# A two-stack block on one Trainium2 core: attention scores issued ahead of the last pair's transposes, a product by pairs, and the recurrent layer's output product with its attention half first

## Chip, cores and metric

The kernel runs on one core of a Trainium2 chip. The metric is device time of one execution in microseconds (us); lower is better. The engines are named as in the profile: PE (TensorE), DVE (VectorE), ACT (ScalarE), POOL (GpSimd), SP (SyncE, here the queue that loads weights). About 0.2% (3 us) is what the measurement can tell from no change.

## The reference, cut to what matters

One sequence of 256 tokens, 1024 features, passes through a first stack of two layers. 16 learned tokens are then put in front (272 tokens) and a second stack follows: a recurrent layer with windowed attention, a feed-forward layer, a state-space layer, a feed-forward layer. Everything is float32. The change touches the mixing part of the first stack's layers and the recurrent layer:

```python
def first_block(x, ...):                      # two layers
    for l in range(DEPTH):
        proj = h @ w_in[l]                    # 1024 -> q, kv, gates, gla q/k/v/gate, pool inputs
        mixed = concatenate([
            nsa_mixer(...),                   # 6 query heads, 2 kv groups
            gla_mixer(...),                   # 6 heads of gated linear attention, times silu(og)
            pool_mixer(...)])                 # causal mean windows 2, 4, 8, 16
        h = layer_norm(ALPHA * h + mixed @ w_out[l], ...)
        ...
def nsa_mixer(q, kv, gates, ...):
    def compress(t, p, w1, w2):               # 15 blocks of 32 tokens
        hid = gelu(tb.reshape(B, G, n_cmp, 32 * 64) @ w1)
        return hid @ w2
    o = gate0 * softmax(q kc') vc + gate1 * softmax(q ks') vs + gate2 * softmax(q kw') vw
def griffin_swa_mixer(u, ...):                # the recurrent layer
    # gates x recurrence (rg_lru) beside windowed attention of 16 query heads
    # y = concatenate([gelu(gate) * rg_lru(conv(xr)), attention]) @ w_out
```

The selected branch takes every block at this length, so that it is plain causal attention, as the window branch is.

## The kernel before, in words

**Numbers and weights.** A float32 operand is kept as two float16 parts, a high and a low one, and a product of weights and operand is three matmuls for a block of 128 x 128 weights and up to 272 tokens: high x high, high x low, low x high (`split_matmul`, L656 to L658). Transposes, scores and values of the attentions are float32 matmuls. Weights stream through slots of 128 x 2048: SP loads a raw slot (four of them), ACT writes its high part (`high_part`, L1403), DVE its low part (`low_part`, L1969). Four split slots exist, so slot n+4 can be split only when the product of slot n is done. Such a split takes both engines in turn. The places where each engine splits the next slot are written out by hand as `give(n)`, `compression(n)` or by `product`.

**First stack, one layer.** The input product has 22 tiles of 128 outputs. Twelve or so come first; then PE's program weaves the rest into the attention. The attention works on six units p = 0 to 5 (three pairs of heads by two halves of 128 queries; units 3 to 5 see 256 keys and cost about twice as much). Unit p takes: `scores(p)` on PE (L950), `maxima(p)` on DVE (L2074, L2076), `exps(p)` on ACT (L1497), `weigh(p)` on DVE (L2082, L2085, L2087: one over the sum, times the branch's gate, times the probabilities), `turn(p)` on PE (transposes, L967), `copy_pt(p)` on ACT (L1506), `values(p)` on PE (L983), `copy_out(p)` on ACT (L1511). Scores live in banks 6 and 7 of PSUM, so scores(p+1) must wait for exps(p). Between them stand `compressed_hidden` (128 pairs of small matmuls for both compressed inputs), `compressed_keys`, `compressed_scores`, `compressed_turn` (L924), `pooled_out` (L992, then POOL's scaling of the residual, L2754) and the last input tiles T_PU (pooling) and T_OG (output gate of the linear attention). PE's order is turn(p), then scores(p+1), then a tile, then values(p).

**Output product and norm of a layer.** `out1` has eight tiles in four slots of two. The first four tiles are computed abreast, one row block of the operand after the other in `OUT1_ORDER`, so that work can begin before the last operand rows are there; the others follow tile by tile. The layer norm's sums are matmuls with a matrix of means (`mean_of`, L734), fed by DVE's evacuation of the tiles (L2010).

**Recurrent layer.** PE's program weaves 26 input tiles, 16 recurrence gates (`lru_gate`) and windowed attention of seven units (`scores`, `turn` L1184, `values`). DVE has for each unit `biased` (bias and maxima), `weight` and `mixed_low`; ACT has `exps`, `copy_turned`, `mixed_high`. The recurrence itself is one scan over 128 x 2176 on DVE (L2482), and `gated_out`, `gated_low` bring its result into the operand of the output product `out_g`, which has K = 16 row blocks: recurrence in the first eight, attention in the last eight. Its first four tiles are computed abreast over all 16 row blocks, and need four split slots at once. Tiles 4 to 7 follow.

## Time and profile before

| | |
|---|---|
| median of 3 runs | 1625.9 us (1624.11 to 1626.73) |
| profiled execution | 1623.0 us |
| its span in the trace | 1620.8 us |
| mean granted clock of PE | 0.932 |
| busy: PE, DVE, ACT, POOL | 1425.7, 1091.2, 819.6, 503.1 us |

The span is what the trace covers; 2.2 us of the profiled execution lie outside it. Busy times are sums of an engine's own work; an engine that is less busy may still be the one that others wait for, which the chain of waits tells. The granted clock is given in parts of 2.4 GHz: 1.00 is 2.4 GHz, 0.50 is 1.2 GHz. Line numbers are those of the kernel before.

### The profile page before, as it was taken

The numbers are of one execution on the slowest core, as the hardware profiler recorded it, in microseconds if no ns is written. First come the engines' busy times: TensorE is split into PE (matmuls) and PEld (weight loads), VectorE is DVE, ScalarE is ACT, GpSimd is POOL, SyncE is SP. The second block draws the span as 40 slices with busy tenths as digits, with TensorE's granted clock in tenths as the row PEclk, the third lists the DMA queues.
The fourth block names the chain that finished last, engine by engine and source line by source line (L and its number), as shares of the span: only waits on it lengthen the run. The fifth ranks groups of instructions, "written<-read, shape, count | busy, mean of one in ns | idle before, by whom it ended". The sixth has DMA issues, their size and how long they took to land.

```text
span 1620.8 us, 29305 instructions
## 1 busy us (share of the span) xinstructions
PE 1425.7 (88%) x12532; PEld 1190.8 (73%) x12532; DVE 1091.2 (67%) x1430; ACT 819.6 (51%) x1210; POOL 503.1 (31%) x390
## 2 busy tenths in 40 slices
PE   6988799989867999969878799997966986979997
PEld 4766688878746888857657688885845775868886
DVE  4864786566666774567846788657883666779863
ACT  5554454345463444447755555544661337555652
POOL 0132796131314991214200366301000111027630
PEclk9987899999979999989989899998986898989999
DMA  8530466545222566525324265552551122436650
GB/s 322 183 105 27 153 212 206 182 152 183 88 96 79 183 208 206 180 70 169 110 99 157 104 209 176 189 192 77 166 170 50 44 64 101 140 108 222 198 193 27
DMA packets 35697, 234.90 MB, mean 145 GB/s; under 512 B 4720, under 2 KB 6768, under 8 KB 8816
## 3 DMA queue, kind: packets, MB, share of 16 engines
q1 hardware_dynamic: 35568, 233.03, 42.0%
q8 instruction: 99, 1.62, 0.4%
q14 instruction: 30, 0.25, 0.0%
HBM read 231.97 MB, written 1.05 MB: 144 GB/s over the span
## 4 chain that ended last, share of the span: by engine, by line
PE 68%; DVE 15%; ACT 8%; issue 5%; DMA 1%; POOL 1%; SPq 0%; DVEq 0%; ACTq 0%; POOLq 0%
PE psum L656 20%; PE psum L657 20%; PE psum L658 20%; DVE low L1969 5%; ACT high L1403 3%; PE psum L734 2%; DVE arena L2331 2%; ACT arena L1497 1%; DMA raw<-stream 1%; PE psum L967 1%; DVE arena L2076 1%; POOL arena L2784 1%; PE psum L950 1%; DVE m L2029 1%; PE psum L1328 0%
## 5 line engine op out<-in xcount | busy, mean ns | idle before, releaser
L656 PE MATMUL psum<-u,high 128*128 128x256 f16 (+3 forms) x2296 | 644.2, 281 | 79.2 <-DVE u L2249 28.4
L1969 DVE SCALAR_TENSOR_TENSOR low<-raw,high 128x2048 f16<-128x2048 f32 (+3 forms) x230 | 522.9, 2280 | 231.0 <-ACT high L1403 230.9
L657 PE MATMUL psum<-u,high 128*128 128x256 f16 (+3 forms) x2296 | 643.4, 280 | 0.5 <-issue 0.5
L658 PE MATMUL psum<-u,low 128*128 128x256 f16 (+3 forms) x2296 | 642.5, 280 | 0.0
L1403 ACT ACTIVATE high<-raw 128x2048 f16<-128x2048 f32 (+3 forms) x230 | 415.2, 1811 | 136.8 <-PE psum L658 127.8
L656 PE MATMUL psum<-arena,high 128*128 128x256 f16 (+2 forms) x1136 | 314.8, 277 | 17.2 <-DVE low L1969 12.0
L656 PEld LDWEIGHTS psum<-u,high 128*128 128x128 f16 (+1 forms) x2296 | 228.3, 99 | 137.0 <-issue 82.9
L657 PE MATMUL psum<-arena,high 128*128 128x256 f16 (+2 forms) x1136 | 314.9, 277 | 0.0
L658 PE MATMUL psum<-arena,low 128*128 128x256 f16 (+2 forms) x1136 | 314.9, 277 | 0.0
L658 PEld LDWEIGHTS psum<-u,low 128*128 128x128 f16 (+1 forms) x2296 | 229.1, 100 | 37.1 <-issue 0.7
L657 PEld LDWEIGHTS psum<-u,high 128*128 128x128 f16 (+1 forms) x2296 | 228.6, 100 | 36.2 <-issue 0.9
L2711 POOL TENSOR_TENSOR arena<-arena 128x256 f16<-128x256 f32 (+1 forms) x108 | 168.8, 1563 | 8.5
L2709 POOL TENSOR_TENSOR arena<-arena 128x256 f32<-128x256 f32 (+1 forms) x108 | 129.2, 1196 | 111.4 <-DVE arena L2347 111.4
L2331 DVE SCALAR_TENSOR_TENSOR arena<-psum,par,arena 128x271 f32<-128x271 f32 (+3 forms) x296 | 142.5, 492 | 27.9 <-ACT arena L1688 13.7
L656 PEld LDWEIGHTS psum<-arena,high 128*128 128x128 f16 x1136 | 112.1, 99 | 36.2 <-DVE low L1969 12.9
L1389 ACT ACTIVATE arena<-psum 128x256 f32<-128x256 f32 (+3 forms) x138 | 52.1, 384 | 165.2 <-PE psum L658 125.9
L657 PEld LDWEIGHTS psum<-arena,high 128*128 128x128 f16 x1136 | 112.1, 99 | 16.8
L658 PEld LDWEIGHTS psum<-arena,low 128*128 128x128 f16 x1136 | 112.2, 99 | 16.2
L1688 ACT ACTIVATE arena<-psum,par 128x272 f32<-128x272 f32 (+1 forms) x88 | 49.4, 570 | 94.8 <-PE psum L658 93.3
L2784 POOL TENSOR_TENSOR arena<-arena 128x512 f32<-128x512 f32 x16 | 20.3, 1271 | 232.6 <-ACT arena L1908 232.6
L2719 POOL TENSOR_TENSOR m<-m,rstd 128x272 f32<-128x272 f32 (+1 forms) x12 | 11.1, 928 | 201.1 <-ACT rstd L1434 201.1
L2236 DVE TENSOR_TENSOR arena<-arena 128x256 f16<-128x256 f32 x64 | 46.6, 749 | 12.2 <-ACT arena L1389 12.1
(319 smaller groups left out, 1420.2 us busy)
## 6 DMA issues: line engine op xcount, KB each, us to landing
raw<-stream SPq DMA_DIRECT2D x208, 1024.0 KB, 4.8
raw<-stream SPq DMA_DIRECT2D x8, 768.0 KB, 4.3
con<-consts SPq DMA_DIRECT2D x1, 1746.0 KB, 12.3
raw<-stream SPq DMA_DIRECT2D x3, 512.0 KB, 3.7
raw<-stream SPq DMA_DIRECT2D x2, 712.0 KB, 5.9
h<-x_t SPq DMA_DIRECT2D x1, 1024.0 KB, 5.7
out_t<-h SPq DMA_DIRECT2D x4, 256.0 KB, 2.4
raw<-stream SPq DMA_DIRECT2D x1, 640.0 KB, 3.8
```

Of the source, the lines that this page charges most:

```text
L656: pe.matmul(out, w_hi, x[0], start=start, stop=False)
L657: pe.matmul(out, w_hi, x[1], start=False, stop=False)
L658: return pe.matmul(out, w_lo, x[0], start=False, stop=stop)
L1389: tell(act.activation(dst, bank(BANK[g], 0, n, rows), func, scale=scale / W_SCALE), *evac_value(g))
L1403: tell(act.activation(high[:, at:at + w], raw[:, off:off + w], ACT.Copy, scale=W_SCALE), high_ready if half != 0 else None)
L1688: tell(act.activation(buf[:, i % GATED, 0:outputs], bank(BANK[g], ahead, ahead + outputs), ACT.Identity, scale=pcol(f"ffn_w{l}", 2 * 2 * F ...
L1969: tell(dve.scalar_tensor_tensor(low[:, at:at + w], raw[:, off:off + w], W_SCALE, high[:, at:at + w], ALU.mult, ALU.subtract), split_ready ...
L2236: tell(dve.tensor_tensor(f1_hi[:, t, :], f_relu[:, t % 4, :], f_relu[:, t % 4, :], ALU.mult), fh_ready)
L2331: ins = dve.scalar_tensor_tensor(dst[:, lo:outputs], bank(BANK[g], at, at + n), weight(taps_in_all - 1 - back), dst[:, lo:outputs], ALU.mu ...
L2709: tell(pool.tensor_tensor(tmp[:, t % 2, 0:n], a[:, t % depth, 0:n], b[:, t % depth, 0:n], ALU.mult))
L2711: tell(pool.tensor_tensor(lo[:, t, 0:n], tmp[:, t % 2, 0:n], hi[:, t, 0:n], ALU.subtract), f_ready)
L2784: tell(pool.tensor_tensor(cd[:, q % 2], e2[:, q % 2], over(xbc[:, 24 + g, t0:t0 + n], 4), ALU.mult), cd_ready)
```

## The change

It changes the written orders of all engines in three places, and some of the work.

1. First stack: scores(p+1) stand ahead of turn(p). `compressed_hidden` is cut into its two inputs; the remaining tiles stand elsewhere, and all T_OG tiles use bank 0; the attention's output of units 3 to 5 uses bank 1. On ACT and DVE, exps(p+1), maxima(p+1) and the splits follow the new order. Gelu of the compressed hidden layer and Silu of the output gate are computed from Tanh with small DVE operations.
2. `out1`: the operand's parts have a home of their own (`g_hi`, `g_lo`), the first two tiles are abreast instead of four, the shift of the mean follows tile 2, and slots are split after each pair of tiles.
3. Recurrent layer: places of recurrence gates, exponentials, splits and of the scan change; the rows of `out_g` are reordered so that the attention stands in row blocks 0 to 7 and the recurrence in 8 to 15, and its slots hold tiles [0, 1] and [2, 3] with eight row blocks each.

```diff
-OUT1_BANKS = [0, 1, 6, 7, 2, 3, 0, 1]
+OUT1_BANKS = [0, 7, 6, 1, 2, 3, 0, 7]
-OUT1_ORDER = [6, 7, 3, 4, 5, 0, 1, 2]
+OUT1_ORDER = [3, 4, 6, 7, 5, 0, 1, 2]
@@ griffin_mix_rows
-    rows = list(range(D))
-    return rows + [D + (g * SWA_J + j) * HD + i for j in range(SWA_J) for g in range(2) for i in range(HD)]
+    rows = [D + (g * SWA_J + j) * HD + i for j in range(SWA_J) for g in range(2) for i in range(HD)]
+    return rows + list(range(D))
@@ slots of the stream
+            if name == "out_g" and i == 0:
+                for k0 in (0, 8):
+                    for both in ([0, 1], [2, 3]):
+                        steps.append((slot(name, 8 * 2 * P, k0, 8, tuple(both)), both, k0, 8))
+                i = 4
+                continue
@@ PE, first stack
                 one(T_PU)
+                scores(1)
                 values_to_tokens()
-                compressed_hidden()
+                turn(0)
+                compressed_hidden(0)
+                scores(2)
+                values(0)
+                turn(1)
+                compressed_hidden(1)
+                scores(3)
+                values(1)
+                turn(2)
                 one(T_PU + 1)
-                turn(0)
-                scores(1)
+                compressed_keys()
+                scores(4)
+                values(2)
+                compressed_scores()
+                turn(3)
                 one(T_OG)
-                values(0)
-                compressed_keys()
-                turn(1)
-                scores(2)
+                scores(5)
+                values(3)
+                turn(4)
                 one(T_OG + 1)
-                values(1)
-                compressed_scores()
...
+                compressed_turn(0)
+                values(4)
+                compressed_turn(1)
+                turn(5)
+                pooled_out()
                 one(T_OG + 2)
...
-                product(f"out1_{l}", x_at, ..., S, shift, late, OUT1_ORDER)
+                product(f"out1_{l}", lambda k: (g_hi[:, k, :], g_lo[:, k, :]), ..., S, shift, late, OUT1_ORDER, pairs=1)
@@ DVE, first stack
                 maxima(0)
                 weigh(0)
+                maxima(1)
...
+                give(7)
+                weigh(1)
+                maxima(2)
                 give(8)
+                low_part(matrices[f"cmp_{l}_0"] + SPLIT)
+                weigh(2)
...
+                tell(dve.scalar_tensor_tensor(t15, h15, GELU_CUBE, h15, ALU.mult, ALU.mult))
+                tell.settle()
+                tell(dve.scalar_tensor_tensor(t15, t15, 1.0, h15, ALU.add, ALU.mult), hid_summed)
+                maxima(3)
+                dve.wait_ge(hid_ready, l + 1)
+                tell(dve.scalar_tensor_tensor(h15, t15, 1.0, h15, ALU.add, ALU.mult), hid_gated)
@@ ACT, first stack
-                tell(act.activation(hid[...], hid[...], ACT.Gelu_apprx_tanh, scale=1.0 / W_SCALE), hid_ready)
-                act.preload_act_table_set("natural_log_exp_and_others")
+                tell(act.activation(hid_tanh[...], hid_tanh[...], ACT.Tanh, scale=GELU_ROOT), hid_ready)
@@ PE, recurrent layer
                 scores(0)
+                one(GQ[4])
                 for n in LRU_ORDER[8:11]:
                     lru_gate(n)
...
                 scores(1)
                 one(GQ[6])
+                for n in LRU_ORDER[14:16]:
+                    lru_gate(n)
                 one(GQ[7])
                 turn(0)
...
-                for step in steps[:4]:
-                    await_slot(step[0])
-                    for j in step[1]:
-                        bank_free(prod["first"] + j)
-                pe.wait_ge(sw_out, 5)
+                for j in range(4):
+                    bank_free(prod["first"] + j)
+                pe.wait_ge(sw_out, len(SWA_UNITS))
                 for half in range(2):
+                    for step in steps[2 * half:2 * half + 2]:
+                        await_slot(step[0])
                     for k in range(8 * half, 8 * half + 8):
-                        if k % 4 == 0:
-                            pe.wait_ge(y_split, min(3, 1 + k // 4))
-                        for step in (steps[half], steps[2 + half]):
+                        if half and k % 4 == 0:
+                            pe.wait_ge(y_split, k // 4 - 1)
+                        for step in steps[2 * half:2 * half + 2]:
@@ ACT, recurrent layer
-                recurrence_gates(8, 11)
                 exps(0)
                 query(4)
-                recurrence_gates(11, 14)
+                recurrence_gates(8, 11)
                 give(6)
                 query(5)
+                recurrence_gates(11, 14)
+                exps(1)
+                query(6)
                 recurrence_gates(14, 16)
@@ DVE, recurrent layer
-                biased(3)
-                tell(dve.tensor_tensor_scan(flat(gmix_a), flat(a_sc), flat(th), 0.0, ALU.mult, ALU.add))
...
                 mixed_low(4)
                 weight(6)
+                tell(dve.tensor_tensor_scan(flat(gmix_a), flat(a_sc), flat(th), 0.0, ALU.mult, ALU.add))
+                mixed_low(5)
                 give(11)
+                mixed_low(6)
```

**What stands where, three places.** Line numbers of the changed kernel differ: its scores are L958, turns L975, values L989, compressed turns L933, pooled product L998, low parts L1977, maxima L2083 and L2085, weigh L2091 to L2096.

PE in the first stack, before: compressed turns, then turn(3) (L967, eight transposes), scores(4) (L950), values(3) (L983), the pooled product (L992), turn(4), scores(5), values(4).

```order
L983 MATMUL psum<-arena 64x128 x4
L924 MATMUL psum<-con,arena 15x128 x8
L967 MATMUL psum<-con,arena 128x128 x8
L950 MATMUL psum<-arena 128x256 x4
L924 MATMUL psum<-con,arena 15x128 x4
L983 MATMUL psum<-arena 64x128 x8
L992 MATMUL psum<-m,misc 64x256 x4
L967 MATMUL psum<-con,arena 128x128 x8
L950 MATMUL psum<-arena 128x256 x4
L983 MATMUL psum<-arena 64x128 x8
```

PE at the same place after the change: scores(5) (L958), values(3) (L989), turn(4) (L975), then the tile T_OG+1 (24 matmuls of L666 to L668, left out), compressed turns (L933), values(4), turn(5) and the pooled product (L998).

```order
L958 MATMUL psum<-arena 128x256 x4
L989 MATMUL psum<-arena 64x128 x8
L975 MATMUL psum<-con,arena 128x128 x8
...
L933 MATMUL psum<-con,arena 15x128 x8
L989 MATMUL psum<-arena 64x128 x8
L933 MATMUL psum<-con,arena 15x128 x4
L975 MATMUL psum<-con,arena 128x128 x8
L998 MATMUL psum<-m,misc 64x256 x4
```

Scores(5) moved in front of turn(4), and the pooled product from between values(3) and turn(4) to behind turn(5).

DVE in the first stack, before: weigh(0) (L2082, L2085, L2087), a low part (L1969), maxima(1) (L2074, L2076), weigh(1), the next low part.

```order
L2082 RECIPROCAL arena<-arena 128x4
L2085 TENSOR_TENSOR arena<-arena 128x4
L2087 TENSOR_TENSOR arena<-arena 128x4x128
L1969 SCALAR_TENSOR_TENSOR low<-raw,high 128x2048
L2074 TENSOR_TENSOR psum<-psum,con 128x2x256
L2076 TENSOR_REDUCE arena<-psum 128x4
L2082 RECIPROCAL arena<-arena 128x4
L2085 TENSOR_TENSOR arena<-arena 128x4
L2087 TENSOR_TENSOR arena<-arena 128x4x128
L1969 SCALAR_TENSOR_TENSOR low<-raw,high 128x2048
```

DVE after the change: maxima(1) (L2083, L2085) stand before, and behind weigh(1) and maxima(2) two low parts (L1977) stand ahead of weigh(2).

```order
L2094 TENSOR_TENSOR arena<-arena 128x4
L2096 TENSOR_TENSOR arena<-arena 128x4x128
L2083 TENSOR_TENSOR psum<-psum,con 128x2x256
L2085 TENSOR_REDUCE arena<-psum 128x4
L1977 SCALAR_TENSOR_TENSOR low<-raw,high 128x2048 x2
L2091 RECIPROCAL arena<-arena 128x4
L2094 TENSOR_TENSOR arena<-arena 128x4
L2096 TENSOR_TENSOR arena<-arena 128x4x128
```

The low part that stood behind weigh(0) is now part of the two in front of weigh(2); maxima no longer wait behind it.

DVE in the recurrent layer, before: unit 3's biases (L2399) and maxima (L2402), then the scan (L2482, 128x2176), then a low part, mixed_low(1) (L2428) and weight(3) (L2420, L2422).

```order
L2399 SCALAR_TENSOR_TENSOR m<-con,psum 128x128 x8
L2402 TENSOR_REDUCE arena<-m 128x8
L2412 TENSOR_TENSOR arena<-arena,lnv 128x8
L2414 TENSOR_TENSOR arena<-par,arena 128x8
L2482 SCALAR_TENSOR_TENSOR arena<-arena 128x2176
L1969 SCALAR_TENSOR_TENSOR low<-raw,high 128x2048
L2428 TENSOR_TENSOR arena<-psum,arena 128x2x128
L2420 TENSOR_TENSOR arena<-arena 128x8
L2422 RECIPROCAL arena<-arena 128x8
```

DVE after the change: weight(6) (L2446, L2448), then the scan (L2521) between mixed_low(4) and the last low parts (L2454 is mixed_low, L1977 a low part).

```order
L2446 TENSOR_TENSOR arena<-arena 128x2
L2448 RECIPROCAL arena<-arena 128x2
L2521 SCALAR_TENSOR_TENSOR arena<-arena 128x2176
L2454 TENSOR_TENSOR arena<-psum,arena 128x2x128
L1977 SCALAR_TENSOR_TENSOR low<-raw,high 128x2048
L2454 TENSOR_TENSOR arena<-psum,arena 128x8x16
L2459 TENSOR_TENSOR arena<-arena 128x1088 x2
```

The scan moved from behind unit 3's maxima to behind the last unit's weight.

## Rows read from the trace of the kernel before

**Rows 1.** Page, part 4: shares of the chain that ended last, by engine.

```profile
PE 68%; DVE 15%; ACT 8%; issue 5%; DMA 1%; POOL 1%; SPq 0%; DVEq 0%; ACTq 0%; POOLq 0%
```

**Rows 2.** Windows by stage: length; busy PE, PEld, DVE, ACT, POOL (count); granted clock; DMA share; GB/s.

```profile
72.62:141.42 68.80, 53.86 (x644) 41.86 (x641) 42.73 (x68) 40.09 (x97) 16.41 (x10) 0.83 0.27 93
141.42:174.34 32.92, 29.38 (x216) 23.71 (x214) 14.76 (x18) 12.17 (x13) 6.29 (x6) 0.91 0.26 87
414.98:483.45 68.47, 51.49 (x630) 39.89 (x628) 42.58 (x66) 40.08 (x97) 16.40 (x10) 0.85 0.28 93
...
756.93:836.54 79.61, 61.55 (x487) 45.64 (x487) 60.96 (x95) 61.39 (x136) 15.64 (x9) 0.90 0.35 120
```

**Rows 3.** Windows at the lower granted clock, columns as in rows 2.

```profile
97.20:100.60 3.40, 3.40 (x18) 2.45 (x17) 2.99 (x3) 0.43 (x3) 3.32 (x2) 0.50 0.26 41
110.90:117.70 6.80, 5.43 (x25) 3.51 (x24) 4.17 (x5) 4.29 (x8) 0.00 (x0) 0.50 0.23 58
124.50:131.30 6.80, 5.88 (x32) 4.33 (x32) 4.76 (x4) 2.14 (x5) 1.09 (x1) 0.50 0.45 145
134.70:145.00 10.30, 10.14 (x65) 8.12 (x66) 5.15 (x15) 5.84 (x12) 0.00 (x0) 0.50 0.00 0
...
827.70:841.30 13.60, 6.50 (x34) 4.16 (x35) 6.92 (x7) 6.44 (x9) 0.00 (x0) 0.50 0.42 147
865.20:872.00 6.80, 5.30 (x24) 3.56 (x25) 6.76 (x6) 6.53 (x9) 0.00 (x0) 0.50 0.64 231
```

**Rows 4.** TensorE's waits, layer 0's attention, then layer 1's (total, times, longest).

```profile
PE psum L967 <- DVE arena L2087: 10.7, 3, 5.1
...
PE psum L967 <- DVE arena L2087: 12.8, 4, 5.1
```

**Rows 5.** The chain in layer 0's attention: start, us, what.

```profile
89.69 1.28 ACT L1577
...
121.56 2.32 DVE arena L2085
...
125.19 1.97 PE psum L967 x8
127.15 2.03 PE psum L950 x8
...
133.38 0.17 DVE arena L2085
...
134.86 1.97 PE psum L967 x8
```

**Rows 6.** The same chain: the two halves of a weight split.

```profile
93.92 1.93 ACT high L1403
...
95.87 3.02 DVE low L1969
```

**Rows 7.** Line L2754: ns min/median/max, first and last start.

```profile
L2754 POOL TENSOR_SCALAR m<-h x2: 5381/5382/5384, 120.2 to 464.3; 128x2048 f32<-128x2048 f32 x2
```

**Rows 8.** The chain in layer 0's output product.

```profile
162.67 2.81 DVE low L1969
```

**Rows 9.** Timeline of DVE behind the last values of layer 0.

```profile
142.25 1.09 DVE L1994 TENSOR_TENSOR u<-arena,u 128x256 f16<-128x256 f32 x3
```

**Rows 10.** TensorE's waits, recurrent layer, 757 to 840 us.

```profile
PE psum L656 <- DVE low L1969: 6.6, 2, 5.1
PE psum L1184 <- ACT arena L1750: 4.6, 1, 4.6
PE psum L1184 <- ACT arena L1752: 4.5, 1, 4.5
```

**Rows 11.** The chain at the recurrent layer's scan.

```profile
795.67 4.60 DVE arena L2482
```

**Rows 12.** TensorE's waits, recurrent output product, 840 to 900 us.

```profile
PE psum L656 <- DVE low L1969: 5.4, 1, 5.4
```

283 lines of the change are left out of this document (133 added, 150 removed).

## Prediction

> **What bounds the kernel now.** I read four views, in this order. First the page's chain that ended last: TensorE (PE) holds 68% of it, DVE 15%, ACT 8% and issue 5% [rows 1]. So time can be won only where PE waits or where it runs at the lower level of its clock. Then the same quantities by stage [rows 2]. In layer 0 of the first stack the attention stretch takes 68.80 us with 53.86 us of PE busy, and layer 1 takes 68.47 us with 51.49: PE idles 14.9 and 17.0 us. The output product and its norm take 32.92 us with 29.38 busy, so 3.5 idle. In the recurrent layer the gates, the windowed attention and the first matmuls of its output product take 79.61 us with 61.55 busy. The granted clock is 0.83 to 0.91 in these stretches: it is not only idle time that is lost.
>
> Third, the stretches in which the granted clock stands at 0.50, which is 1.2 GHz where 1.00 is 2.4 GHz [rows 3]. Each follows a wait of PE. In layer 0's attention they hold 3.40 + 5.43 + 5.88 us of PE busy and about 6.6 of the last row's 10.14 (the part before 141.42): 21.3 us. A matmul takes twice as long there, so up to 10.6 us are lost; I count 9.8, since the first and last matmuls of a stretch belong to the other level. The work of this attention is then 53.9 - 9.8 = 44.1 us at the full clock.
>
> Fourth, who ends PE's waits [rows 4] and the chain in one pair's round [rows 5]. Of layer 0's 14.9 us, 10.7 end with DVE's weigh (the scaling of the probabilities, L2087), all of them in front of a turn (L967); in layer 1 it is 12.8. The chain shows why. A turn starts at 125.19 and takes 1.97, then the next pair's scores take 2.03 (127.15), and only then can maxima, exponentials and weigh of that pair begin, so the next turn starts at 134.86: 9.67 us for a round in which PE has 4.0 us of turn and scores on the chain. In the late rounds no projection tile is left to fill the gap.
>
> **What the change does, part by part.**
>
> *First stack, attention (twice).* The scores of pair p+1 are issued in front of turn(p), and the interleaved projections and compressed parts are spread so that each round has one. The softmax of pair p+1 (from the end of the scores at 129.2 to the turn at 134.86 in the round shown, 5.6 us of maxima, exponentials and weigh) then runs beside values, turn and a tile of the pair before. Nothing is added on PE: the same matmuls, so 44.1 us of work. What takes the place of the old waits? Weight splits are queued on DVE in front of two of the weighs. In layer 0 ACT's half of a split takes 1.93 us now and DVE's 3.02 [rows 6]. Weigh(1) stands behind one split: I allow 1.1 us for turn(1). Weigh(2) stands behind two, the second of which needs ACT's half, which needs the slot that the first compressed product frees: 4 us, about one split of both engines (4.95) less what PE has to do meanwhile. For compressed keys, the last turns and the pooled product I add 3, together 8 where 14.9 stood. One gap of 4 us can bring the lower clock again; I allow 4 us of loss, where 9.8 is lost now. So 44.1 + 8 + 4 = 56.1 instead of 68.80: 12.7 won. In layer 1, with the same share of loss (9 us of 51.49), 42.5 + 12 = 54.5 instead of 68.47: 14.0. Together 26.7; I take 27. The ends: no wait and no low clock would give 14.9 + 9.8, less 5 that no order can hide, 20 a layer; with every round still waiting two thirds of what it waits now and the clock unchanged it is 4 a layer.
>
> *Table loads.* Gelu and Silu are replaced by Tanh with small operations on DVE, so that two of ACT's four table loads per layer go. One of them stood on the chain, 1.28 us at 89.69 [rows 5]. In the new order PE has other work at that place, so I count nothing extra, and up to 2.6 a layer as part of the upper end. The added DVE operations are about eight of four to thirty elements a row and three of 256; nearest row: the small one of 0.2 us on this chain, so some 2 us of DVE time, beside the last rounds, in which DVE waits.
>
> *POOL beside DVE.* POOL's scaling of the residual takes 5.4 us right after the pooled product, from 120.2 on [rows 7]. There it meets weigh(4): a four-element operation took 2.32 us (121.56), where the same operation takes 0.17 in the next round (133.38) [rows 5]. After the change the pooled product stands behind turn(5), so no weigh can meet it, and 2.1 us of today's wait go with it. It will meet the gating of the linear attention and the low halves of the operand instead. These have some 4 us of cover (compressed output, values(5), first five rows of the product). Price if the cover fails: up to 3 us a layer; I take 0. The Trainium skill's "GPSIMD Engine Reference", section "Key points", says that GpSimd shares its SBUF interfaces with VectorE, with contention for VectorE instructions with two SBUF inputs. That rule speaks against this placement, since the gating operations have two such inputs; the slow operation of the trace agrees with it, and by the rule alone the sum would be up to 6 us worse in the two layers.
>
> *First stack, output product (twice).* It now goes one pair of tiles abreast and then tile by tile, the shift of the mean comes after tile 2, and weights are split after every pair. At most the 3.5 us of idle go, and the low clock up to 145.0 (3.6 us, half of it lost, 1.8) [rows 3]: 5.3 a layer. Today DVE's half of a split stands on the chain there with 2.81 us, ahead of the evacuation of the last tiles [rows 8]. A new risk: with two tiles abreast instead of four, the five rows that are ready early cover 30 matmuls instead of 60 (216 take 29.38 us [rows 2], so about 3.5 us of them at the full clock). The last low halves end at 143.34, 1.9 us after the last values [rows 9], so they stay hidden. I take 5.0; ends 2 and 5.3. Two layers: 10.
>
> *Recurrent layer, middle.* The longest waits for turns and values there are 4.6 and 4.5 us [rows 10]. ACT's exponentials now come ahead of recurrence gates 14 and 15, whose product must be evacuated before turn(0) may use the bank; I get a stall of about 4.2 in front of turn(0) in place of the 4.5. With PE up to 2.6 us behind the old times at turn(2) and the scan of 4.60 (now in the middle of the weighs, at 795.67 [rows 11]) moved behind the last weigh, it recovers, and I count 0.
>
> *Recurrent layer, output product.* Its rows are reordered so that the attention half comes first. The first half now needs only two split slots, not four, and none of the recurrence. Today PE waits 5.1 us, the longest of the two for splits [rows 10], and starts at 836.54, where the last stretch of [rows 2] ends, at the lower clock, up to 841.3 [rows 3]. I get a start at about 831.7: 4.8 won and 2.4 of clock. The second half needs the recurrence, with the scan now late: its operand is ready at about 839.4 and its weights at 841.7 by my count, the first half ends at 843.0. This is close. Behind it the weights of tiles 4 and 5 can be split as soon as the first half is done, not after all four tiles: the wait of 5.4 [rows 12] goes, and the low clock after it (5.30 us of busy, half lost, 2.7). Sum 4.8 + 2.4 + 5.4 + 2.7 = 15.3. Two of these steps rest on margins of 1.3 and 3.6 us, so I take 11. Ends: -2 (the middle loses 2.6 and the second half waits for the scan) and 16.
>
> **The sum.** 27 + 10 + 11 = 48. The profiled execution took 1623.0 us (span 1620.8), so 1575.0; its time is 2.9 below the median of 1625.9, to which I apply the same difference: 1578. Bounds: 2 x (4 + 2) - 2 = 10 and 2 x (20 + 5.3) + 16 = 67.
>
> **Rivals.**
> *The full gain* (forecast): 40 to 60 won, 1566 to 1586; chance 0.57. For it: the waits are nearly all for one thing, which the new order takes off the path.
> *More than 60*, the clock at its full level through both attentions: under 1566; 0.08.
> *The weight splits take the place of the softmax.* Each round then keeps some 2 us of wait and its low clock; attention gives 4 to 5 a layer instead of 13. 9 + 10 + 11 = 30, time 1596; span 1586 to 1606; 0.20. For it: in layer 0 a split stood on the chain with 4.95 us, and the low stretches follow gaps of at most 5.1 us, while one of 4 remains by my count. The Trainium skill's "TensorE: Matmul & The Clock Gate", section "Why this matters for your kernels", asks for no idle gaps between bursts of matmuls, or the clock goes down to half; the stretches at 0.50 agree.
> *The recurrent layer gives nothing*: the second half waits for scan and gating, whose 4.60 us now come last. 37 won, 1589, span 1586 to 1592; 0.09. Against it: DVE is busy 60.96 of the 79.61 us, so it has room to catch up.
> *Slower.* Both halves of a split (1.93 + 3.02) come in front of every weigh, and the 24 matmuls beside them run at the lower clock: 4.95 + 1.3 in each of ten rounds, 62 lost against 48 won, 1640. It decides from 4.8 us a round on. Against it: only two of five rounds have a split queued in front. 0.04.
> *The change does nothing*, since the rounds are bound by DVE's own work: DVE is busy 42.73 of 68.80 us [rows 2], so hardly; 0.02.
>
> **How the numbers follow.** 0.2% (3 us) is about what a measurement of this kernel tells from no change. Faster 0.94, same 0.02, slower 0.04. The range takes the forecast, the recurrent rival, nearly half of the rival of the splits and a third of those over 60: 1563 to 1597.
>
> **What would show it.** Right: the attention stretches at 54 to 58 us with PE busy 46 to 49; the waits for weigh down from 10.7 and 12.8 to under 6, most of them in front of turn(1) and turn(2); no slow four-element operation in a weigh; the recurrent product starting five us earlier, with no wait for a split in its third pair. Wrong: a new long wait of TensorE for weigh or for recurrence gates 14 and 15; a granted clock that stays under 0.9 in the attentions; a wait for the gated recurrence in the middle of its product.

## The result, and the profile after

The changed kernel takes 1560.7 us (median of 4 runs, 1559.8 to 1562.0) against 1625.3 of the kernel before in the same runs: a ratio of 0.9603 (0.9591 to 0.9615). That is 64.6 us faster, where 48 were forecast, and 2.3 us below the lower end of the range. The profiled execution has a span of 1557.8 us, 63.0 less than before.

Where the 63.0 us come from is read from the starts of TensorE's groups of matmuls in both timelines. A stage ends where the next one's first matmul starts; "to the next product" includes the norm behind the output product.

| stage | before | after | won | forecast |
|---|---|---|---|---|
| up to the attention, layer 0 | 72.69 | 71.33 | 1.4 | 0 |
| attention, layer 0 | 68.80 | 52.46 | 16.3 | 13 |
| output product to the next product, layer 0 | 38.23 | 31.72 | 6.5 | 5 |
| feed-forward, layer 0 | 167.01 | 168.04 | -1.0 | 0 |
| input product of layer 1, up to its attention | 68.32 | 66.05 | 2.3 | 0 |
| attention, layer 1 | 70.30 | 51.40 | 18.9 | 14 |
| output product to the next product, layer 1 | 36.28 | 31.71 | 4.6 | 5 |
| feed-forward, layer 1, and input of the recurrent layer | 235.95 | 235.59 | 0.4 | 0 |
| recurrent layer, scores(0) to its output product | 78.96 | 77.74 | 1.2 | 4.8 |
| recurrent layer, output product | 53.76 | 43.70 | 10.1 | 10.5, with 4.3 held back from both |
| everything behind it | 730.5 | 728.1 | 2.4 | 0 |

The page of the changed kernel, part 4, the chain that ended last by engine:

```profile
PE 74%; DVE 13%; ACT 6%; issue 5%; POOL 1%; DMA 1%; SPq 0%; DVEq 0%; ACTq 0%; POOLq 0%
```

TensorE (PE) holds 74% of the chain where it held 68%, with 21 us less of busy time (1404.3 against 1425.7 for the same matmuls; the mean granted clock rose from 0.932 to 0.948): the rest of the 63.0 us is wait. By stage (length; busy PE, PEld, DVE, ACT, POOL with counts; granted clock; DMA share; GB/s), the answer to [rows 2]:

```profile
71.33:123.80 52.47, 48.37 (x642) 38.95 (x642) 44.26 (x70) 37.29 (x96) 15.34 (x10) 0.87 0.36 121
123.80:149.90 26.10, 26.09 (x214) 22.48 (x214) 17.71 (x23) 12.59 (x15) 6.57 (x7) 1.00 0.41 134
389.61:441.01 51.40, 46.91 (x642) 37.67 (x642) 44.06 (x70) 36.83 (x96) 15.45 (x10) 0.90 0.37 124
707.66:786.05 78.39, 63.02 (x487) 46.40 (x487) 54.15 (x90) 53.57 (x130) 19.92 (x9) 0.93 0.31 108
786.05:829.75 43.70, 43.41 (x373) 36.50 (x374) 31.14 (x33) 28.18 (x35) 0.00 (x0) 1.00 0.52 180
```

The last column but two is the granted clock. The two attentions have 4.1 and 4.5 us of idle PE where there were 14.9 and 17.0. Both output products run at a granted clock of 1.00 without a gap, and so does the recurrent output product. What PE waits for in layer 0's attention, then in layer 1's (total, times, longest), the answer to [rows 4]:

```profile
PE psum L904 <- issue: 1.7, 1, 1.7
PE psum L975 <- DVE arena L2096: 1.3, 1, 1.3
PE psum L958 <- DVE arena L2168: 0.5, 1, 0.5
...
PE psum L975 <- DVE arena L2096: 3.7, 2, 2.3
PE psum L958 <- ACT arena L1506: 0.3, 1, 0.3
```

L975 is the turn, L2096 weigh. The waits of 10.7 and 12.8 us in front of the turns are now 1.3 and 3.7. The 1.7 us without a releaser stand among the small matmuls of `compressed_hidden`. In the recurrent layer, up to the output product and at its start:

```profile
PE psum L1172 <- POOL m L2795: 5.6, 3, 3.6
PE psum L1172 <- ACT arena L1733: 4.5, 1, 4.5
PE psum L1189 <- ACT arena L1760: 2.0, 1, 2.0
...
PE psum L666 <- DVE arena L2454: 1.2, 1, 1.2
```

L1172 is the turn of this layer, L1189 its values. (Their lines before are L1167 and L1184: both waits at L1184 in [rows 10] stood in front of values, not of a turn.) The 5.4 us of [rows 12] are gone, and the 4.5 us in front of turn(0) are there as forecast (4.2). Grown is the first row: PE waits for POOL, at most 3.6 us at a time, where it waited 1.1 us in all before. The last row is what is left in front of the output product, where 5.1 us stood [rows 10].

The lower clock did not go away. In layer 0's attention it stands from 85.4 to 99.0 us (columns as above):

```profile
86.00:90.00 4.00, 3.63 (x101) 3.31 (x102) 3.81 (x4) 2.32 (x11) 0.00 (x0) 0.50 0.78 266
90.00:93.60 3.60, 1.87 (x43) 1.66 (x40) 1.93 (x1) 2.29 (x2) 0.00 (x0) 0.50 0.74 250
93.60:97.00 3.40, 3.40 (x21) 2.22 (x18) 3.14 (x12) 1.49 (x2) 0.00 (x0) 0.50 0.72 217
97.00:100.70 3.70, 3.70 (x27) 2.78 (x24) 3.67 (x5) 2.54 (x10) 0.00 (x0) 0.73 0.31 128
```

It begins during the wait of 1.3 us in front of turn(1) and holds over the wait of 1.7. The wait need not be its cause: the kernel with five edits, below, has the lower level at the same place and no wait there. The attention's busy time of 48.4 us is 4.3 above the 44.1 that I worked out for the full clock.

### The profile page after: what moved, and what is told of

It reads as the page before. It is cut to its first block, busy times and chain, and to the rows that moved or that the text cites. A ratio compares the mean times of both kernels' runs of the same rounds, so it can differ in the third digit from the quotient of the medians.

```text
span 1557.8 us, 29313 instructions
## 1 busy us (share of the span) xinstructions
PE 1404.3 (90%) x12532; PEld 1181.0 (76%) x12532; DVE 1091.9 (70%) x1442; ACT 815.7 (52%) x1210; POOL 506.7 (33%) x390
## 3 DMA queue, kind: packets, MB, share of 16 engines
q1 hardware_dynamic: 35568, 233.03, 43.7%
## 4 chain that ended last, share of the span: by engine, by line
PE 74%; DVE 13%; ACT 6%; issue 5%; POOL 1%; DMA 1%; SPq 0%; DVEq 0%; ACTq 0%; POOLq 0%
PE psum L666 22%; PE psum L667 22%; PE psum L668 22%; DVE low L1977 4%; ACT high L1408 2%; PE psum L744 2%; DVE arena L2357 2%; ACT m L1748 1%; POOL arena L2808 1%; PE psum L975 1%; DVE m L2038 1%; DMA raw<-stream 1%; DVE m L2425 1%; PE psum L1333 0%; PE psum L958 0%
## 5 line engine op out<-in xcount | busy, mean ns | idle before, releaser
L666 PE MATMUL psum<-u,high 128*128 128x256 f16 (+4 forms) x2168 | 606.7, 280 | 78.4 <-DVE u L2275 28.4
L1977 DVE SCALAR_TENSOR_TENSOR low<-raw,high 128x2048 f16<-128x2048 f32 (+3 forms) x230 | 517.9, 2257 | 226.6 <-ACT high L1408 226.4
L667 PE MATMUL psum<-u,high 128*128 128x256 f16 (+4 forms) x2168 | 606.0, 280 | 0.0
L668 PE MATMUL psum<-u,low 128*128 128x256 f16 (+4 forms) x2168 | 605.4, 279 | 0.0
L666 PE MATMUL psum<-arena,high 128*128 128x256 f16 (+2 forms) x1264 | 347.5, 275 | 8.2 <-DVE arena L2654 5.2
L667 PE MATMUL psum<-arena,high 128*128 128x256 f16 (+2 forms) x1264 | 347.5, 275 | 0.0
L668 PE MATMUL psum<-arena,low 128*128 128x256 f16 (+2 forms) x1264 | 347.5, 275 | 0.0
L666 PEld LDWEIGHTS psum<-u,high 128*128 128x128 f16 (+2 forms) x2168 | 215.2, 99 | 132.3 <-issue 80.1
L668 PEld LDWEIGHTS psum<-u,low 128*128 128x128 f16 (+2 forms) x2168 | 215.7, 99 | 33.8
L667 PEld LDWEIGHTS psum<-u,high 128*128 128x128 f16 (+2 forms) x2168 | 215.3, 99 | 33.9 <-issue 0.9
L666 PEld LDWEIGHTS psum<-arena,high 128*128 128x128 f16 x1264 | 123.8, 98 | 28.2 <-issue 7.9
L667 PEld LDWEIGHTS psum<-arena,high 128*128 128x128 f16 x1264 | 123.9, 98 | 17.9
L668 PEld LDWEIGHTS psum<-arena,low 128*128 128x128 f16 x1264 | 124.0, 98 | 16.8
L1394 ACT ACTIVATE arena<-psum 128x256 f32<-128x256 f32 (+3 forms) x138 | 51.9, 382 | 161.3 <-PE psum L668 121.8
L2743 POOL TENSOR_TENSOR m<-m,rstd 128x272 f32<-128x272 f32 (+1 forms) x12 | 11.1, 927 | 184.3 <-ACT rstd L1439 184.3
```

Source lines behind the costliest of these rows:

```text
L666: pe.matmul(out, w_hi, x[0], start=start, stop=False)
L667: pe.matmul(out, w_hi, x[1], start=False, stop=False)
L668: return pe.matmul(out, w_lo, x[0], start=False, stop=stop)
L1394: tell(act.activation(dst, bank(BANK[g], 0, n, rows), func, scale=scale / W_SCALE), *evac_value(g))
L1977: tell(dve.scalar_tensor_tensor(low[:, at:at + w], raw[:, off:off + w], W_SCALE, high[:, at:at + w], ALU.mult, ALU.subtract), split_ready ...
```

## The experiments

**The two halves of the change apart.** The recurrent layer's part alone:

> The recurrent layer's part of the change alone, first stack as before. If the two parts do not touch each other, the time is 11.3 us under the kernel before (78.39 and 43.70 us in the changed kernel's two stretches against 79.61 and 53.77), so about 1614. Rival: the parts help each other through the clock (the 2.4 us that the changed kernel won in stretches that it did not touch); then this kernel wins 13 or more, or 9 or fewer.

Measured 1609.8 us, ratio 0.9911 (0.9895 to 0.9928): 14.8 us, above the 11.3 expected. The first stack's part alone:

> The first stack's part alone, recurrent layer as before. Theory: 24.4 us in the first and 24.6 in the second layer, so 49 under the kernel before, about 1576.5. Prediction on record had 37 for it. Rival: part of the 49 belongs to clock levels that differ from run to run; then 44 or less.

Measured 1572.5 us, ratio 0.9683 (0.9668 to 0.9697): 52.1 us. The halves add up to 66.9 where both together give 64.6, so they do not help each other; the spans give 13.0 and 50.7, which is 63.7 against 63.0. The trace of the recurrent part alone has 11.2 us of its 13.0 between scores(0) and the end of the output product, and 2.4 behind it, in code that is the same (0.5 are lost ahead). The same 2.4 us appear in the changed kernel, and not with the first stack's part alone (its stages behind the recurrent layer take what they took before). They are not a property of the recurrent part either: from the first matmul of the next feed-forward layer to the end it is 713.8 us before and 711.3 in the changed kernel, and 713.1 in two kernels below that have the same recurrent part (the turns ahead of the scores, and four tiles abreast). What they are is seen at the start of that feed-forward layer. Before, two windows from its first matmul on:

```profile
904.27:908.00 3.73, 3.73 (x17) 2.54 (x18) 3.59 (x9) 1.17 (x3) 0.00 (x0) 0.50 0.00 0
908.00:912.00 4.00, 4.00 (x30) 3.08 (x29) 3.85 (x9) 1.41 (x4) 0.00 (x0) 0.80 0.01 4
```

And the changed kernel's, from the same matmul on:

```profile
843.72:847.45 3.73, 3.73 (x21) 2.68 (x22) 3.59 (x9) 1.17 (x3) 0.00 (x0) 0.62 0.00 0
847.45:851.45 4.00, 4.00 (x37) 3.37 (x36) 3.86 (x9) 1.41 (x4) 0.00 (x0) 1.00 0.01 4
```

PE is busy all the time in both. Before, the lower level lasts through the first window and into the second (0.80); in the changed kernel it ends inside the first (0.62). That is 2.5 us less of the lower level, and 1.2 us of time; the state-space layer behind it is shorter by 1.2 us as well, again by shorter stretches at the lower level. The wait ahead of the feed-forward layer was the same 8.5 us. The level comes back at another distance from the first matmul, in kernels that differ only by what was done before.

**The order of turn and scores alone.** The changed kernel with each turn ahead of the scores again, the tiles left in place:

```diff
@@ PE, and so for the other pairs up to turn(4), scores(5)
-                scores(1)
                 values_to_tokens()
                 turn(0)
+                scores(1)
                 compressed_hidden(0)
-                scores(2)
                 values(0)
                 turn(1)
+                scores(2)
@@ ACT, and so for the other pairs
-                exps(1)
                 copy_pt(0)
+                exps(1)
```

> The changed kernel with one thing undone: each turn(p) ahead of scores(p+1) again, on ACT copy_pt(p) ahead of exps(p+1), and the tiles left where the change has them. If the scores' place is what wins the attention stretch (waits of 10.7 to 12.8 us for weigh), the waits come back at nearly every turn, 3 to 4 us a round in the two or three rounds without enough other work: 10 to 15 us a layer with the lower clock, 20 to 30 in all, time 1581 to 1591. Rival: the even spread of the tiles and the shorter softmax path are what wins; then at most 8 us in all, up to 1569.

Measured 1591.0 us, ratio 0.9794 (0.9780 to 0.9809), 30 us slower than the changed kernel. The two attentions' windows and the waits in front of the turns:

```profile
71.40:134.10 62.70, 50.72 (x641) 39.95 (x640) 43.93 (x67) 33.20 (x88) 14.73 (x10) 0.84 0.30 102
404.45:465.36 60.91, 49.99 (x640) 39.23 (x640) 43.22 (x67) 32.90 (x88) 14.90 (x10) 0.83 0.31 105
```

```profile
PE psum L975 <- DVE arena L2096: 10.2, 3, 3.8
...
PE psum L975 <- DVE arena L2096: 9.5, 4, 3.8
```

The waits are back at 10.2 and 9.5 us, and the granted clock is down again (0.84 and 0.83). The attentions take 62.7 and 60.9 us up to the end of their last values: 10.2 and 9.5 us of the gain belong to the place of the scores. From there to the next product it also became 5 us longer (36.7). Behind the last values of layer 0:

```profile
134.10:138.00 3.90, 0.61 (x5) 0.51 (x5) 1.71 (x5) 3.77 (x9) 0.45 (x1) 0.94 0.00 0
138.00:144.00 6.00, 6.00 (x44) 4.80 (x43) 4.85 (x9) 3.92 (x7) 0.00 (x0) 0.76 0.01 3
```

PE is busy 0.6 of 3.9 us, and then runs partly at the lower clock. What it waits for, and what DVE and POOL did a little earlier:

```profile
PE psum L666 <- ACT arena L1394: 3.3, 1, 3.3
129.25 3.86 DVE L2244 SCALAR_TENSOR_TENSOR arena<-arena 128x256 f32<-128x256 f32 x1
129.00 5.55 POOL L2778 TENSOR_SCALAR m<-h 128x2048 f32<-128x2048 f32 x1 [13.24 <-PE psum L998]
```

The releaser, L1394 on ACT, is the evacuation of the last input tile, T_OG+2, whose bank 0 the product's first tile uses. It is late because ACT had stood 3.82 us for DVE's gating of the linear attention, and one operation of that gating (L2244) took 3.86 us beside POOL's scaling of the residual, where it takes 0.42 in the changed kernel. Layer 1 shows the same 3.86 and 3.3 us. So the total is at the upper end of what was expected, but a third of it is another mechanism: in this order POOL's pass happens to meet the gating, which the chain of waits shows and no run tried apart. To the place of the scores itself belong some 20 of the 30 us. Open stayed what the other 6.1 and 9.4 us of the attentions are.

**POOL's scaling of the residual beside weigh(4).** In layer 1 before, POOL and then DVE (start, length, instruction):

```profile
464.28 5.38 POOL L2754 TENSOR_SCALAR m<-h 128x2048 f32<-128x2048 f32 x1 [18.95 <-PE psum L992]
```

```profile
465.09 2.86 DVE L2085 TENSOR_TENSOR arena<-arena 128x4 f32<-128x4 f32 x1
467.99 1.23 DVE L2087 TENSOR_TENSOR arena<-arena 128x1024 f32<-128x1024 f32 x1
```

A DVE operation on four elements takes 2.86 us while POOL's pass runs. To price this alone, the kernel before got one wait more on POOL:

```diff
                 pool.wait_ge(pool_done, l + 1)
+                pool.wait_ge(attn_p, 6 * l + 6)
```

> The kernel before with one wait more on POOL: its scaling of the residual (5.38 us) begins only when weigh(5) is done, instead of beside weigh(4). The prediction took 2.1 us of weigh(4) in layer 0 for this meeting and counted its end as part of the gain. Theory: the four-element operation of weigh(4) (2.32 us in layer 0, 2.86 in layer 1) takes 0.17 again, the wait of 5.1 us in front of turn(4) shrinks by as much, and the scaling now lies beside the gating and the low halves of the operand, of which it can delay those of the last heads: 2 to 5 us faster than the kernel before. Rival: the delay of the low halves in front of the output product takes it all back: no change within 1 us.

Measured 1619.2 us, ratio 0.9968 (0.9956 to 0.9980): 5.5 us faster than the kernel before with this line alone (3 to 7 by the interval), at the upper end of the theory. The operation in weigh(4) of layer 0, and then POOL's pass and the operations of DVE that it meets now:

```profile
122.65 0.16 DVE L2085 TENSOR_TENSOR arena<-arena 128x4 f32<-128x4 f32 x1
```

```profile
132.66 5.38 POOL L2755 TENSOR_SCALAR m<-h 128x2048 f32<-128x2048 f32 x1 [30.75 <-DVE arena L2087]
```

```profile
133.18 4.08 DVE L2225 TENSOR_TENSOR arena<-arena 128x256 f32<-128x256 f32 x3 [0.69 <-ACT arena L1615]
```

0.16 us instead of 2.31. The three products with the output gate take 4.08 us beside the pass, which is late enough to cost less. The attentions became 2.2 and 3.4 us shorter; the output product's stage became 1.9 us shorter in layer 0 and 1.9 longer in layer 1. So of the 6.1 and 9.4 us that the order of turn and scores leaves, 2.2 and 3.4 are POOL, if its price in the kernel before holds for the changed one. The rest (3.9 and 6.0) lies with what else the first stack's part moves: the spread of the tiles, the places of the splits, the small operations around Tanh. I did not try these apart.

In the changed kernel the pass meets the low halves of the operand, as the prediction said. DVE, then POOL:

```profile
118.97 4.65 DVE L2003 TENSOR_TENSOR arena<-arena 128x256 f16<-128x256 f32 x4 [0.22 <-ACT arena L1433]
```

```profile
118.69 5.38 POOL L2778 TENSOR_SCALAR m<-h 128x2048 f32<-128x2048 f32 x1 [6.61 <-PE psum L998]
```

Four operations take 4.65 us. PE shows no wait there: the cover was enough.

**The splits in front of weigh(2).**

```diff
-                low_part(matrices[f"cmp_{l}_0"] + SPLIT)
                 weigh(2)
+                low_part(matrices[f"cmp_{l}_0"] + SPLIT)
```

> The changed kernel with DVE's weigh(2) ahead of the split of the slot behind the first compressed product, instead of behind it. The prediction allowed 4 us a layer for the wait of turn(2) that this split brings. The trace of the changed kernel shows none in layer 0 and 2.35 us in layer 1. Theory: the split costs what layer 1 shows, with some of the lower clock behind it: 1 to 4 us faster in all. Rival (the prediction's): 8 us faster. Second rival: the slot is then split later, and the compressed product that needs it or the tile behind it waits: no change or slower.

Measured 1557.6 us, ratio 0.9585 (0.9571 to 0.9599), 3 us under the changed kernel, with intervals that just overlap. In the attentions of the two traces 0.6 and 1.4 us are won. The turns' wait in layer 1 is 1.1 instead of 3.7:

```profile
PE psum L975 <- DVE arena L2096: 1.1, 1, 1.1
```

So in the changed kernel the split does not cost the 4 us a layer that the prediction charged; the theory of this run fits. The next run shows where the 4 us are.

**Where DVE splits give(6) and give(7).**

```diff
                 tell(dve.tensor_tensor(tb_lo, tb, tb_hi, ALU.subtract), tb_split)
+                give(6)
...
                 rotate(2)
-                give(6)
+                give(7)
...
-                give(7)
                 weigh(1)
```

> The changed kernel with DVE's splits give(6) and give(7) at their old places (ahead of the linear attention's sums and behind the last rotation). Theory: the wait of 1.1 us in front of the linear attention's outputs comes back in each layer, and the 1.3 us of wait in front of turn(1), behind which give(7) stands in the changed kernel, goes: within 1.5 us of the changed kernel. Rival: the gain ahead of the attention (1.4 and up to 2.3 us a layer) was all of give(6), and nothing comes back at turn(1): 3 us slower.

Measured 1558.9 us, ratio 0.9593 (0.9578 to 0.9607), within what can be told from the changed kernel. Waits of layer 0, from 60 us on:

```profile
PE psum L975 <- DVE arena L2096: 4.1, 1, 4.1
PE psum L867 <- DVE arena L2160: 1.1, 1, 1.1
```

The 1.1 us in front of the linear attention's outputs (L867) are back in both layers, so these were give(6). The 1.3 us in front of turn(1) are gone, as the theory had it. New is the wait of 4.1 us, and it stands in front of turn(2), where the changed kernel had none; layer 1 has 2.8 us at the same place:

```profile
PE psum L975 <- DVE arena L2096: 2.8, 1, 2.8
```

Yet layer 0's attention is shorter (49.6 us instead of 52.5). The 1.7 us without a releaser are gone, and the stretch ran at a granted clock of 0.97:

```profile
72.60:122.20 49.60, 44.79 (x641) 36.28 (x642) 41.50 (x69) 36.96 (x96) 15.68 (x10) 0.97 0.32 107
```

PE's busy time of 44.8 us is close to what the prediction had worked out for the full clock (44.1), and the 4.1 us at turn(2) are the 4 us that it had charged there. At the full clock PE comes to turn(2) early and waits; in the changed kernel it comes late, and the same delay of weigh(2) is hidden. A single wait of 4.1 us cost less than 1.3 and 1.7 with the lower clock beside them.

**Table loads.** The Tanh of the compressed hidden layer is replaced by Gelu on the same input:

```diff
-tell(act.activation(hid_tanh[...], hid_tanh[...], ACT.Tanh, scale=GELU_ROOT), hid_ready)
+tell(act.activation(hid_tanh[...], hid_tanh[...], ACT.Gelu_apprx_tanh, scale=GELU_ROOT), hid_ready)
```

> The changed kernel with the Tanh of the compressed hidden layer replaced by Gelu on the same input (the result of this branch is then another one), so that two table loads a layer come back on ACT, 1.28 us each, between exps(2) and exps(3). The prediction counted nothing for the loads in the new order and 2.6 a layer as its upper end. Theory: ACT waits 1.3 us on either side of that place, so at most one load is seen: 0 to 3 us slower in all. Rival: both delay exps(3) and with it turn(3): 5 us slower.

Measured 1559.8 us, ratio 0.9603 (0.9587 to 0.9619): no difference. ACT at that place:

```profile
95.25 1.28 ACT L1592 ACT_TABLE_LOAD   x1
96.55 0.23 ACT L1592 ACTIVATE sq<-sq 128x30 f32<-128x30 f32 x1
96.79 1.28 ACT L1506 ACT_TABLE_LOAD   x1
98.26 0.47 ACT L1506 ACTIVATE arena<-psum,arena 128x256 f32<-128x256 f32 x1 [0.18 <-DVE arena L2085]
```

Two loads of 1.28 us each, and the exponentials behind them still wait 0.18 us for DVE. As predicted, the loads cost nothing in the new order.

**Four tiles abreast and the splits as before in the output product.**

```diff
-OUT1_BANKS = [0, 7, 6, 1, 2, 3, 0, 7]
+OUT1_BANKS = [0, 7, 6, 2, 1, 3, 0, 7]
-                    if j == (2 if m % 2 == 0 else 1):
+                    if j == 1:
-                product(f"out1_{l}", ..., OUT1_ORDER, pairs=1)
+                product(f"out1_{l}", ..., OUT1_ORDER)
@@ ACT and DVE, the same with low_part
-                    if n == 1 and not name.startswith("out1"):
+                    if n == 1:
                         high_part(i - 1 + SPLIT)
-                    if (n or name.startswith("out1")) and not (hold and ...):
+                    if n and not (hold and ...):
```

> The changed kernel with the first stack's output product as before in its form: four tiles abreast, mean's shift behind tile 1, slots split behind the second pair. Its operand's order and home stay new. The changed kernel needs 31.7 us from the last values to the next product where the kernel before needs 38.2 and 36.3. Theory: the splits behind every pair are what removes the waits (3.5 us a layer), and the rest is the clock: 4 to 7 us slower in all. Rival: it is all the clock, which stays at its full level because the attention ends without a gap: no more than 1.5 us slower.

Measured 1569.7 us, ratio 0.9660 (0.9646 to 0.9675), 9 us slower. The stages take 37.1 and 35.8 us instead of 31.7, at a full clock from their start. The wait, the same in both layers:

```profile
PE psum L744 <- DVE m L2019: 3.2, 2, 2.2
```

So the form of the product is worth 5.4 and 4.1 us by itself, more than expected. Most of it is wait (3.6 us a layer with a small one for ACT); in layer 0 the lower level, from 151.3 to 154.8 us, stands behind it.

**Recurrence gates ahead of exps(1) on ACT.**

```diff
-                exps(1)
                 query(6)
                 recurrence_gates(14, 16)
+                exps(1)
```

> The changed kernel with ACT's exponentials of unit 1 behind recurrence gates 14 and 15 instead of ahead of them. PE waits 4.5 us for these gates in front of turn(0) now. Theory: that wait goes, but ACT is full from exps(1) to exps(2) (the square root, the decays, a split and a table load), so exps(2) moves by 1.3 us only and the rest comes back as a wait there: 1 to 2 us faster. Rival: the wait is the bound and 4 us are won.

Measured 1558.8 us, ratio 0.9592 (0.9578 to 0.9606), within what can be told from the changed kernel; the stretch from scores(0) to the output product took 76.8 instead of 77.7. The wait of 4.5 us is gone, and another has taken its place, in front of values:

```profile
PE psum L1189 <- ACT arena L1760: 4.4, 3, 3.9
```

That fits the theory that ACT is full between exps(1) and exps(2).

**The scan and POOL's multiplication.** The changed kernel's wait of 3.6 us for POOL stands in front of turn(6). DVE, then POOL:

```profile
773.33 4.67 DVE L2521 TENSOR_TENSOR_SCAN arena<-arena 128x2176 f32<-128x2176 f32 x1
```

```profile
773.49 5.39 POOL L2795 TENSOR_TENSOR m<-m,arena 128x544 f32<-128x544 f32 x1 [3.09 <-DVE arena L2448]
```

The last multiplication (128x544) lasts 5.39 us, until 0.9 us behind the end of the scan. With the scan behind mixed_low(5):

```diff
-                tell(dve.tensor_tensor_scan(flat(gmix_a), flat(a_sc), flat(th), 0.0, ALU.mult, ALU.add))
                 mixed_low(5)
+                tell(dve.tensor_tensor_scan(flat(gmix_a), flat(a_sc), flat(th), 0.0, ALU.mult, ALU.add))
```

> The changed kernel with the recurrence's scan on DVE behind mixed_low(5) instead of ahead of it. In the changed kernel POOL's multiplication for the last unit (128x544) took 5.39 us beside the scan (4.67), where it takes 1.10 in the kernel before, and PE waited 3.6 us for it in front of turn(6). Theory: POOL cannot work beside this scan; with the scan begun later the multiplication takes 1.1 again, the wait goes and the time falls by 3 to 4.5 us against the changed kernel (1556 to 1558). Rival: the multiplication is slow for its own shape or the scan only moves the wait to the product's second half: no change within 1 us.

Measured 1558.7 us, ratio 0.9597 (0.9583 to 0.9611). The wait in front of turn(6) is gone, and one of 3.7 us stands in front of the output product, for mixed_low(6), which the scan now delays:

```profile
PE psum L666 <- DVE arena L2454: 3.7, 1, 3.7
```

The product starts 2.4 us earlier in the stage, and its first half runs partly at the lower clock (46.1 us instead of 43.7). So the mechanism was right and the gain was not. With the scan behind mixed_low(6) too:

```diff
-                tell(dve.tensor_tensor_scan(flat(gmix_a), flat(a_sc), flat(th), 0.0, ALU.mult, ALU.add))
                 mixed_low(5)
                 give(11)
                 mixed_low(6)
+                tell(dve.tensor_tensor_scan(flat(gmix_a), flat(a_sc), flat(th), 0.0, ALU.mult, ALU.add))
```

> The changed kernel with the scan behind mixed_low(6), the last attention operation of DVE, so that neither POOL's last multiplication nor mixed_low(5), a split and mixed_low(6) stand beside or behind it. Theory: the wait of 3.6 us for POOL goes as in the kernel with the scan behind mixed_low(5), and the wait of 3.73 us that came there in front of the output product does not come; the product begins 5 us earlier and its second half then waits about 1.4 us for a split. 3 to 5 us faster than the changed kernel, 1556 to 1558. Rival: the recurrence comes too late for the second half, whose wait takes all back: within 1 us of the changed kernel.

Measured 1559.1 us, ratio 0.9591 (0.9577 to 0.9606), again within what can be told from the changed kernel. POOL's multiplication:

```profile
773.28 1.09 POOL L2795 TENSOR_TENSOR m<-m,arena 128x544 f32<-128x544 f32 x1 [3.10 <-DVE arena L2448]
```

1.09 us, and the product starts 4.3 us earlier in its stage (73.45 us behind scores(0) instead of 77.74). It gives back 1.6 us in the product and 2.6 behind it, nearly all of it lower clock: the product's only wait behind its start is the 0.3 us of the changed kernel, and PE's idle time behind the layer differs by 0.4. The rival of a late recurrence did not come.

**All four slots before the first matmul.**

```diff
+                for step in steps[:4]:
+                    await_slot(step[0])
                 for half in range(2):
-                    for step in steps[2 * half:2 * half + 2]:
-                        await_slot(step[0])
```

> The changed kernel with the recurrent layer's output product waiting for all four split slots before its first matmul, as in the kernel before; rows and slots stay in the new order. In the changed kernel the split of the fourth slot ends 10 us behind the product's start. Theory: the start moves by 10 us, the lower clock follows (about 2.4 us), and nothing is given back later, since the wait in front of the third pair of tiles is hidden by the same early splits only if the first half ends first: 8 to 13 us slower. Rival: DVE and ACT are the bound of the stretch and the end moves by less than 5.

Measured 1574.9 us, ratio 0.9690 (0.9674 to 0.9707), 14 us slower, a little over the 8 to 13 expected. One wait of 11.4 us for the fourth split in front of the product:

```profile
PE psum L666 <- DVE low L1977: 11.4, 1, 11.4
```

The start moved by 10.3 us and the product took 2.9 longer at the lower clock. In the new order, that the first half needs only two slots is thus worth more than the whole recurrent part won.

**Put together.** Weigh(2) ahead of its split, the gates ahead of exps(1), the scan last, and give(12) ahead of gated_low:

```diff
@@ beside the three edits above
+                give(12)
                 gated_low(0)
                 gated_low(1)
-                give(12)
```

> The changed kernel with four edits: weigh(2) ahead of its split (measured alone: 2.9 us under the changed kernel by the ratios), recurrence gates 14 and 15 ahead of exps(1) on ACT (1.8 alone), the scan behind mixed_low(6), and the split give(12) on DVE ahead of gated_low. If they add up, 8 to 11 us faster than the changed kernel, 1550 to 1553. Rival: the two edits in the recurrent layer want the same slack of ACT, and only 5 to 6 come.

Measured 1553.2 us, ratio 0.9560 (0.9546 to 0.9574): 7.5 us under the changed kernel and the fastest version measured, between the 8 to 11 of full addition and the rival's 5 to 6. By stages 2.9 us come in the two attentions and 5.4 ahead of the recurrent output product, which gives 1.7 back. Give(12) has no price of its own. With give(6) and give(7) at their old places as a fifth edit:

> The kernel with four edits, and the splits give(6) and give(7) on DVE at their old places as a fifth (1.8 us alone by the ratios, weigh(2) ahead of its split 2.9 alone). Both act on the waits in front of turn(1) and turn(2). Theory: they add up in part, 1 to 3 us under the kernel with four edits: 1550 to 1552. Rival: one takes the slack that the other needs, within 0.7 us of it.

Measured 1554.2 us, ratio 0.9570 (0.9557 to 0.9583), no further gain, which is nearer to the rival. The attention of layer 0 fell from 50.9 to 48.4 us and layer 1's from 50.0 to 49.5, but 1.4 us are lost ahead of layer 0's, and the other stages took 1.7 more. Layer 0's attention, and four microseconds in its run of small matmuls:

```profile
72.80:121.20 48.40, 47.66 (x643) 38.43 (x642) 41.62 (x68) 36.70 (x96) 15.61 (x10) 0.89 0.33 110
86.00:90.00 4.00, 4.00 (x112) 3.56 (x112) 3.90 (x6) 3.79 (x12) 0.00 (x0) 0.50 0.00 0
```

Here PE waits nowhere in this attention for longer than 0.4 us, and still the level is at 0.50 from 85.7 to 95.9 us. The wait of 4.1 us at turn(2) is gone against the kernel with give(6) and give(7) alone, and 2.9 us of busy time came in its place (47.7 against 44.8). The recurrent part alone shows the same without any change to the first stack: from 84.2 to 90.8 us its granted clock is 0.50 with PE busy throughout, where the kernel before has 1.00 in those microseconds.

## Why the prediction missed

The direction and the mechanism were right; the forecast of 48 fell 15 us short. Term by term:

- **Attention, 27 against 35.2.** This is the step that failed: "together 8 where 14.9 stood", the waits left in each layer. 4.1 and 4.5 us were left. Of the 8 us, 1.1 were for turn(1), and 1.3 came in each layer. 4 were for turn(2) behind two splits; layer 0 shows none and layer 1 2.3. The second split was late, but PE was late as well: the lower clock, which I had charged separately, kept it busy. I had charged one delay twice. The run with give(6) and give(7) at their old places shows the other side: there the clock was full, and the 4.1 us stood in front of turn(2). The 3 us "for compressed keys, the last turns and the pooled product" had no row behind them, and 0.9 and 0.7 us came. In layer 0 1.7 us without a releaser came in addition. The clock's term had the right size (4 allowed, 4.3 measured in layer 0), but by luck: I tied it to a gap of 4 us, and the stretch with that gap ran at 0.97, while the one with no wait at all (five edits) ran at 0.89. Layer 1's row of [rows 2] ended ahead of its last values, at 483.45; to their end the stretch takes 70.30 us, so 1.8 us of its length was left out. The 8.2 us are thus 7.4 of waits that did not come and 1.8 of that window, less 0.7 of busy time above what I allowed and 0.3 of rounding.
- **Nothing ahead of the attention, against 1.4 and 2.3.** Give(6) stood in front of the linear attention's sums. The prediction did not price this move at all; 1.1 us of it in each layer is shown by the run with the old places. The rest of layer 1's 2.3 is clock: a lower level that lasted into 361 to 366 us before (0.76) is over in the same matmuls after (1.00).
- **POOL beside DVE.** The 2.1 us in layer 0 were rightly read; in the kernel before the meeting is worth 5.5 us in both layers. That the new meeting with the operand's low halves costs nothing was right too, by the cover; with the turns ahead of the scores the pass fell on the gating instead, and the stage behind took 5 us more in each layer. The rule that spoke against the placement held for DVE's operations (4.65 us for four of them) and cost no time, for the cover. But the same rule stood against the other end of the change, where I didn't apply it: the scan beside POOL's multiplication. The Trainium skill's "GPSIMD Engine Reference", section "Key points", names the sharing without a direction; here both directions were seen.
- **Output product of the first stack, 10 against 11.1.** Right, and for the reason given.
- **Table loads, nothing.** Right, and tried.
- **Recurrent layer, 11 against 11.3.** Right in the sum by luck, and not in its parts. The product gave 10.1 of the 10.5 for it; the earlier start gave 1.2 of 4.8, because of POOL's multiplication. What I had held back for margins (4.3) was lost in another place than I thought, where no rival had it. The rival in which the second half waits for the recurrence did not come: its operand and slots were there in time.
- **Untouched code, 0 against 1.8** (2.4 behind the recurrent layer, 0.4 and -1.0 in the feed-forwards): mostly the length of the lower clock behind waits that did not change.

These make 8.2 + 3.6 + 1.1 + 0.3 + 1.8 = 15.0. The case that came, "more than 60", had a chance of 0.08, with the full clock in both attentions as its condition. That condition was not met (0.87 and 0.90; a clock under 0.9 even stood among the signs of being wrong): the same total came by shorter waits. The range ended too close to the sum on this side: each wait was charged at what its row could cost, none at what was left if PE came late as well.

What stays open: how the 3.9 and 6.0 us of the attentions that belong neither to the order of turn and scores nor to POOL divide among the moved tiles, splits and small operations, and what decides when the clock falls in a run of small matmuls without a wait, and when it comes back.

## What to carry to other kernels

When an engine stalls once a round on a softmax done by others, issue the next round's producer ahead of this round's consumer; here it was worth 10 us a stretch in waits and clock. When you charge a new wait behind a late engine, ask whether the waiting engine is late too by then, and charge one of the two; a wait taken away can also come back in part as busy time at the lower clock. And a long operation of DVE or POOL should be placed by what the other of the two does on short notice: one line that moved a 5.4 us pass out of a softmax was worth 5.5 us, and in an order in which the same pass met the gating, the stage behind took 5 us more in each layer, 3.3 of them in one wait.
